# Attention turns its probabilities at another distance and in another order, and norms and the first up projection are interleaved by chunk

## The reference

```python
# first model, one layer (the context is updated in layer 0 only)
u  = modulate(rms_norm(h, g_norm1), mod[0], mod[1]);  uc = the same of the context
ya = diff_attention(...)                          # 4 heads of differences
yb = mla(...)                                     # 8 heads, latent: queries 64 + 32 rotary
yw = window_gqa(...)                              # 8 heads, window 128, with a sink
h  = h + mod[2] * merge_branches(u, (ya, yb, yw), ...)
u2 = modulate(rms_norm(h, g_norm2), mod[3], mod[4])
h  = h + mod[5] * conv_ffn(u2, w_up, conv_w, conv_b, w_down)

def mla_core(qn, qr, kn, kr, v):
    s = (q_nope . k_nope + q_rope . k_rope) * MLA_SCALE
    p = softmax(s);  return p @ v                 # 768 keys (512 + 256), context queries 256

def window_gqa(...):                              # blocks of 128 queries, keys: context + 3 blocks
    p = softmax_with_sink([s_context, s_band], sink);  return p @ v

def conv_ffn(t, w_up, conv_w, conv_b, w_down):
    a = dwconv(t @ w_up, conv_w, conv_b)          # w_up: 1024 x 5632
    gate, val = split(a);  return (silu(gate) * val) @ w_down

# second model, one layer
h = rmsnorm(x, attn_norm_w);  proj = h @ w_in
x = x + concat(ssd_mixer(...), short conv, nsa_mixer(...)) @ w_out    # 4 attention heads
h = rmsnorm(x, ffn_norm_w);   x = x + (silu(gate) * val) @ ffn_w_down
```

## Time and profile before

| | us |
|---|---|
| median of three runs | 4219.41 (4217.53 to 4221.92) |
| the profiled execution | 4218.24 |
| its span | 4216.5 |
| PE busy | 3872.1 (92% of the span) |
| DVE busy | 2300.0 (55%) |
| ACT busy | 1602.4 (38%) |
| POOL busy | 310.6 (7%) |

### The profile page before, as it was taken

One profiled execution on the slowest core, in us unless ns is written; L12 is line 12 of the kernel. 1 busy time (PEld: TensorE's weight loads), 2 busy tenths in 40 slices (PEclk: granted clock), 3 DMA queues, 4 the chain that ended last, 5 costly groups with the idle time before them and its releaser, 6 DMA issues. The chain is left out here.

```text
span 4216.5 us, 54188 instructions
## 1 busy us (share of the span) xinstructions
PE 3872.1 (92%) x20018; PEld 3044.8 (72%) x20018; DVE 2300.0 (55%) x3968; ACT 1602.4 (38%) x2718; POOL 310.6 (7%) x278
## 2 busy tenths in 40 slices
PE   4988979998999888999899899979899998989998
PEld 3875557776888787865678688856578886657886
DVE  6355567854553474364633556255657625565752
ACT  2245561112442353254632344243444424344431
POOL 0000001111000000100000100104010010400001
PEclk8999999999999999999999999989899999979999
DMA  5200005551223343200022233222023322202332
GB/s 175 61 28 19 1 22 172 193 191 56 95 95 105 99 160 114 77 28 19 1 90 85 78 97 95 99 67 83 13 80 98 97 94 83 80 16 87 98 99 81
DMA packets 86729, 350.83 MB, mean 83 GB/s; under 512 B 9520, under 2 KB 9648, under 8 KB 85680
## 3 DMA queue, kind: packets, MB, share of 16 engines
q1 hardware_dynamic: 72752, 298.53, 22.2%
q0 software_dynamic: 13824, 50.34, 3.6%
HBM read 346.73 MB, written 2.10 MB: 83 GB/s over the span
## 5 line engine op out<-in xcount | busy, mean ns | idle before, releaser
L498 DVE TENSOR_TENSOR split_low<-weight_ring,split_high 128x1024 fp32r<-128x1024 f32 (+2 forms) x460 | 623.0, 1355 | 677.6 <-ACT split_high L490 667.2
L490 ACT ACTIVATE split_high<-weight_ring 128x1024 fp32r<-128x1024 f32 (+2 forms) x474 | 535.0, 1130 | 918.1 <-PE banks L1460 468.8
L1632 PE MATMUL banks<-normed_high,split_high 128*128 128x512 f32 (+1 forms) x1760 | 653.8, 371 | 55.8 <-DVE normed_low L437 36.0
L1632 PE MATMUL banks<-normed_low,split_high 128*128 128x512 f32 (+1 forms) x1760 | 651.3, 370 | 0.0
L1632 PE MATMUL banks<-normed_high,split_low 128*128 128x512 f32 (+1 forms) x1760 | 650.6, 370 | 0.0
L1632 PEld LDWEIGHTS banks<-normed_high,split_high 128*128 128x128 f32 x1760 | 334.4, 190 | 117.5 <-issue 61.7
L1632 PEld LDWEIGHTS banks<-normed_low,split_high 128*128 128x128 f32 x1760 | 334.7, 190 | 55.8
L1632 PEld LDWEIGHTS banks<-normed_high,split_low 128*128 128x128 f32 x1760 | 334.6, 190 | 55.4
L1460 PE MATMUL banks<-hidden_high,split_high 128*128 128x512 f32 (+1 forms) x880 | 325.1, 369 | 8.8 <-DVE split_low L498 8.8
L1460 PE MATMUL banks<-hidden_low,split_high 128*128 128x512 f32 (+1 forms) x880 | 324.5, 369 | 0.0
L1460 PE MATMUL banks<-hidden_high,split_low 128*128 128x512 f32 (+1 forms) x880 | 324.3, 369 | 0.0
(11 more groups left out here) (327 smaller groups left out, 7228.7 us busy)
## 6 DMA issues: line engine op xcount, KB each, us to landing
weight_ring<-in_up SPq DMA_DIRECT2D x220, 512.0 KB, 3.6
weight_ring<-in_down SPq DMA_DIRECT2D x80, 704.0 KB, 4.0
modulation_ring<-in_ada POOLq DMA_DIRECT2D x80, 512.0 KB, 4.7
weight_ring<-in_merge SPq DMA_DIRECT2D x48, 768.0 KB, 4.4
weight_ring<-in_inputs SPq DMA_DIRECT2D x36, 512.0 KB, 3.5
weight_ring<-in_out SPq DMA_DIRECT2D x32, 512.0 KB, 3.6
latents<-in_ada POOLq DMA_DIRECT2D x16, 512.0 KB, 4.7
weight_ring<-in_xbc SPq DMA_DIRECT2D x16, 512.0 KB, 3.6
```

The lines of the kernel that those rows point to most:

```text
L490: act.activation(k.splits[0][:, (n0 + panel) % RING, 0:width], k.slot(n0 + panel)[:, 0:width], ACT.Copy).then_inc(k.high_ready.sem, 1)
L498: dve.tensor_tensor(k.splits[1][:, s, 0:width], k.ring[:, s, 0:width], k.splits[0][:, s, 0:width].bitcast(F32), ALU.subtract).then_inc(k.l ...
L1632: last = pe.matmul(sums(r, half), w, x, start=(c + j == 0), stop=(c == KT - 1 and j == 2))
```

## The change

Three parts.

1. In `norm`, DVE makes the low part of chunk i - 1 right after scaling chunk i (scaled 0, scaled 1, low 0, scaled 2, low 1, ..., scaled 7, low 6, low 7). This holds wherever a norm splits, in both models.
2. `attention` has a new argument. With `one_behind`, given to the latent attention alone, PE turns step t - 1 after the scores of step t, DVE normalises step t - 1 ahead of the maxima of step t, and ACT runs copy(t-1, 0), exponential(t, 0), exponential(t, 1), copy(t-1, 1). Without it the distance stays two, and ACT runs copy(t-2, 0), exponential(t, 0), copy(t-2, 1), exponential(t, 1). The difference attention has one copy per step and stays as it was.
3. `ffn_up` in the first model opens with a tile whose first four chunks go through both panels in turn, then chunks 4 to 7 of the first panel, then of the second. Tiles 0 and 1 are written out ahead of the loop, which runs 10 times for the rest. In the second model tiles 0 and 1 are written out too, in the order as before.

```diff
--- before.py
+++ after.py
@@ -414,6 +414,17 @@
         @block.vector
         def _(dve):
+            def low_part(q):
+                dst = flat[q][2][1]
+                dve.wait_ge(*k.high_ready(ahead + q + 1))
+                high = split[0][q].bitcast(F32)
+                if shifted:
+                    rest = dve.scalar_tensor_tensor(split[1][q], dst, flat[q][2][3](ranges_of[0][0][2]), high,
+                                                    ALU.add, ALU.subtract)
+                else:
+                    rest = dve.tensor_tensor(split[1][q], dst, high, ALU.subtract)
+                rest.then_inc(tile_ready.sem, 1)
+
...
-                for src, dst, gain, _ in group:
+                for i, (src, dst, gain, _) in enumerate(group):
                     for a, b, which in ranges_of[g]:
                         dve.scalar_tensor_tensor(dst[:, a:b], src[:, a:b], gain(which), k.probs[:, 3, a:b],
                                                  ALU.mult, ALU.mult).then_inc(k.scaled_ready.sem, 1)
-            for q, (_, _, (_, dst, _, _)) in enumerate(flat if split else ()):
...
+                    if split and i:
+                        low_part(tiles_before[g] + i - 1)
+            if split:
+                low_part(len(flat) - 1)
@@ -973,7 +978,7 @@
            constants_loaded=16)
-def attention(k, steps, turned, spare, scratch=None):
+def attention(k, steps, turned, spare, scratch=None, one_behind=False):
     nc = k.nc
@@ -982,6 +987,7 @@
     per = 1 if combined else 2
     slots = len(turned)
     groups = [sum(step["last"] for step in steps[:t]) for t in range(U)]
+    behind = 1 if one_behind else 2
@@ -1044,15 +1050,15 @@
-            for t in range(U + 3):
+            for t in range(U + behind + 1):
                 if t < U:
                     score(t)
-                if 2 <= t < U + 2:
-                    turn(t - 2, 0)
-                if t >= 3:
-                    weigh(t - 3)
-                if 2 <= t < U + 2 and per == 2:
-                    turn(t - 2, 1)
+                if behind <= t < U + behind:
+                    turn(t - behind, 0)
+                if t > behind:
+                    weigh(t - behind - 1)
+                if behind <= t < U + behind and per == 2:
+                    turn(t - behind, 1)
         @block.vector
         def _(dve):
@@ -1109,15 +1115,21 @@
-            for t in range(U + 3):
+            def normalise_both(t):
+                if 0 <= t < U:
+                    normalise(t, 0)
+                    normalise(t, 1)
+
+            for t in range(U + behind + 1):
+                if behind == 1:
+                    normalise_both(t - 1)
                 if t < U:
                     maximum(t, 0)
                     maximum(t, 1)
-                if 1 <= t <= U:
-                    normalise(t - 1, 0)
-                    normalise(t - 1, 1)
-                if t >= 3:
-                    store(t - 3)
+                if behind == 2:
+                    normalise_both(t - 1)
+                if t > behind:
+                    store(t - behind - 1)
@@ -1146,14 +1158,17 @@
-            for t in range(U + 2):
-                if t >= 2:
-                    copy(t - 2, 0)
+            for t in range(U + behind):
+                if t >= behind:
+                    copy(t - behind, 0)
                 if t < U:
                     exponential(t, 0)
+                    if behind == 1:
+                        exponential(t, 1)
+                if t >= behind and per == 2:
+                    copy(t - behind, 1)
+                if t < U and behind == 2:
                     exponential(t, 1)
-                if t >= 2 and per == 2:
-                    copy(t - 2, 1)
                 if scratch is not None and t >= 4:
                     square(t - 4)
             for t in range(U - 2, U) if scratch is not None else ():
@@ -1611,27 +1626,53 @@
     @block.tensor
     def _(pe):
-        with pe.Fori(0, FF_TILES // 2) as i:
-            for r in range(2):
+        def chunk(r, half, c):
+            for j, (w, x) in enumerate(triple(split_parts(k, n0, half, c * P), (highs[:, c, :], lows[:, c, :]))):
+                last = pe.matmul(sums(r, half), w, x, start=(c + j == 0), stop=(c == KT - 1 and j == 2))
+            return last
+
+        def sums_free(i, r):
+            if late is None:
+                pe.wait_ge(*k.taps_added(i * 8 + 4 * (r - 1)))
+            else:
+                pe.wait_ge(*k.scaled_ready(i * 4 + 2 * (r - 1)))
+            if late is not None and r == 1:
+                pe.wait_ge(*k.deviation_ready(0))
+
+        def opening_tile():
+            sums_free(0, 0)
+            for c in range(KT // 2):
+                pe.wait_ge(*k.normed_ready(c + 1 - KT))
                 for half in range(2):
-                    pe.wait_ge(*k.low_ready(i * 4 + (2 * r + half + 1)))
...
+                    if c == 0:
+                        pe.wait_ge(*k.low_ready(half + 1))
+                    chunk(0, half, c)
+            for half in range(2):
+                for c in range(KT // 2, KT):
+                    if half == 0:
+                        pe.wait_ge(*k.normed_ready(c + 1 - KT))
+                    last = chunk(0, half, c)
+                last.then_inc(k.product_ready.sem, 1)
+
+        def tile(i, r):
+            for half in range(2):
+                pe.wait_ge(*k.low_ready(i * 4 + (2 * r + half + 1)))
+                if half == 0:
+                    sums_free(i, r)
+                for c in range(KT):
+                    if r + half == 0:
+                        pe.wait_ge(*k.normed_ready(c + 1 - KT))
+                    last = chunk(r % 2, half, c)
+                last.then_inc(k.product_ready.sem, 1)
+
+        if late is None:
+            opening_tile()
+        else:
+            tile(0, 0)
+        tile(0, 1)
+        with pe.Fori(0, FF_TILES // 2 - 1) as i:
+            tile(i, 2)
+            tile(i, 3)
@@ -1844,7 +1885,7 @@
-    attention(k, steps, turned, [latents[:, 0, :], latents[:, 1, :]])
+    attention(k, steps, turned, [latents[:, 0, :], latents[:, 1, :]], one_behind=True)
```

More of the change, by code:

```diff
@@ L431, in _ @@
                                                  ALU.mult, ALU.mult).then_inc(k.scaled_ready.sem, 1)
-            for q, (_, _, (_, dst, _, _)) in enumerate(flat if split else ()):
-                dve.wait_ge(*k.high_ready(ahead + q + 1))
-                high = split[0][q].bitcast(F32)
-                if shifted:
-                    rest = dve.scalar_tensor_tensor(split[1][q], dst, flat[q][2][3](ranges_of[0][0][2]), high,
-                                                    ALU.add, ALU.subtract)
-                else:
-                    rest = dve.tensor_tensor(split[1][q], dst, high, ALU.subtract)
-                rest.then_inc(tile_ready.sem, 1)
+                    if split and i:
+                        low_part(tiles_before[g] + i - 1)
+            if split:
+                low_part(len(flat) - 1)
     squares = 0 if summed else len(flat)
```

14 lines of the change are left out of this document (removed).

## The result

The changed kernel takes 4173.64 us (median of four runs, 4172.29 to 4178.12) against 4218.66 us before in the same comparison: a ratio of 0.9889, interval 0.9877 to 0.9900. That is 45 us less.

What follows compares the result with a forecast made beforehand. TensorE (PE), busy 92% of the span, was taken as the bound, so only its waits pay. -10.6 - 4.0 - 8.8 - 9.1 + 4.0 = -28.5 us gave 4190.5 us; own range 4184 to 4196, 8 in 10 for 4179 to 4205.

Steps and rivals of the forecast that it cites:

- Window attention: Window attention, both layers: second copy ahead of the second exponential removes PE's waits; 10.6 us gained, between 7 and 13.
- Second model's attention: Second model's attention: the copy's new place saves 2.0 of 5.4 us per layer, 4.0 in all, bounds 0 and 7.
- a rival for the clock: Second model's attention: climb to the higher clock some 5 us later per layer, norm openings denser; -20, 4199 us, chance 0.09.
- Latent attention: Latent attention: distance one shortens fill and drain and keeps the clock up; 8.8 us gained, between 1.5 and 10.
- rival d: Latent attention: chain longer than a step's 6.05 us, so all 40 steps pay; +18, 4237 us, chance 0.03.
- the 1.6 us that I had for the clock: Latent attention's fill, per layer: without the second gap the clock stays up, saving an estimated 1.6 us.
- Openings: First model's feed-forward openings and the context's: earlier low parts start PE sooner; 9.1 us gained, between 6 and 11.
- the pairing is what makes this pay: First model's feed-forward opening: one panel at a time would starve PE, two panels paired would not; gain 3.8 us per layer.
- Second model's norms: Second model's norms: interleaving gains nothing and a clock fall costs 2 us per layer; +4 in all, between 0 and +5.
- job 2 would start when it did: Second model, after the first job: the next panel's split lands at about 2790.7, when the first job used to end.
- the fall of the clock in that gap: Second model's first job: a gap of 2 us lowers the clock, ten matmuls or so at double length, +2 us per layer.
- the 7 us of its upper bound: Second model's attention: most that the copy's new place was taken to gain there, 7 us in all.

Runs made afterwards that it cites:

- e10: Kernel before plus one extra 128-column matmul ahead of each turn in the second model's attention; 4212.15 us against 4221.45.
- e9: Changed kernel with distance two in the latent attention, keeping ACT's new order of the copies there; 4185.18 us, ratio 0.9907.
- e7: Changed kernel, but the first model's first feed-forward tile takes one panel after the other, without pairing; 4181.40 us.
- e11: Changed kernel plus one extra 128-column matmul ahead of each turn in the second model's attention; 4176.94 us, ratio 0.9898.
- e3: Changed kernel with the attention function of the kernel before, leaving only the norms by chunk and the opening tile; 4211.96 us, ratio 0.9975.
- e4: Changed kernel, but in the second model's attention only the iteration scoring step 2 has the new copy order, all later ones the old; 4193.60 us.
- e5: Changed kernel, but in the second model's attention the iteration scoring step 2 keeps the old copy order; 4173.69 us.

## Why the prediction was wrong, point by point

- **Window attention**: -9.7 us measured, -10.6 forecast. The anatomy of the earlier trace rows was read rightly. (Three stretches at 2.0 make 6.0, not the 5.8 of the sum.) In layer 1 the waits for the copy shrank by 3.5 us (6.0 to 2.5), less than the 4.8 I took, and the lower clock stood 5.8 us longer than before.
- **Second model's attention**: the step that failed. I priced a wait by its own length ("I take 2.0 of 5.4 per layer") and said of the lower clock only that PE "seldom waits" there, as if it were given. The waits did shrink by about 2 us per layer, but with them the clock's time at the lower level went from 49 to 30 and 26 us, which took another 6.6 and 7.7 us of PE's busy time. The lower clock was a result of the very waits, as e10 shows. So the term that I had at nothing was the clock's part of the gain: 14.3 us over both layers, beside the 3.6 us by which PE's idle time fell, near the 4.0 I had taken for it. I even had a rival for the clock, and gave it the wrong sign: that the climb would come later. (Its sum doesn't come out either: 28.5 less 5 less 1 is 22.5, not 20.)
- **Latent attention**: -8.2 against -8.8. Both ends and the hidden chain (rival d) came out as reckoned. That the clock stays up with the second gap gone is true in thirteen of eighteen fills, and was not in the very profile of layer 0. There the 1.6 us that I had for the clock didn't come, and the rest was 3.4 us where I had 2.6; that the total is near the forecast is in part luck. Read as a price, distance one also guards against falls such as those for which e9's slowest execution paid 5 and 6 us.
- **Openings**: -8.1 against -9.1; waits 3.8, 2.4 and 3.8 us shorter, as worked out, less 0.5 us each in the up projection, which the sum didn't have (0.4 us more lies in the matmuls ahead of the waits, by the cut of the stages). That "the pairing is what makes this pay" was too strong: e7 keeps two thirds without it.
- **Second model's norms**: +1.2 against +4.0. That job 2 would start when it did was right (the wait of 2.11 us); the fall of the clock in that gap, for which I had +2 per layer, didn't come in this profile. Elsewhere it did: in e11, e3 and e4 (layer 1) and in e7 (both layers) the clock fell for 3.4 us behind the same gap of 2.1 us, five of sixteen cases with this order, and the jobs up to the next gap took 1.6 us more. So the mechanism exists and was nearly the size I had given it, but it doesn't come each time.
- **Rivals and range**: no rival let the second model's attention gain more than the 7 us of its upper bound, so the range's lower end of 4179 was 5 us too high. Those bounds, 0 and 7 us, were taken from the waits alone.

## What to carry to other kernels

Where a stage runs at a mean clock well under one and PE has many short waits in it, don't price a wait by its length: count the time at the lower clock as well, and take half of it, the lower level being half of the higher, as the upper bound of what denser work can give back (here 18.8 and 23.2 us less at the lower clock, so 9.4 and 11.6 at most, and 6.6 and 7.7 measured). Read the clock's falls together with the waits, and part cause from company by adding work to PE, not only by taking waits away. Distance one paid where a step is longer than the chain behind its scores (6.05 against 4.8 us); whether it costs where the step is shorter stays open. And when a switch carries two choices with it, as the distance here carries the copy's place, compare with the kernel that shares the other one.

## What the runs showed of the hardware

More work made a stage shorter: 48 extra matmuls of 128 columns gave 5.4 and 4.9 us back. And the same instructions don't always meet the same clock. The latent attention with distance one, the same code in nine kernels, took 126.3 us in layer 0 where the clock never fell (five profiles) and 131.9 where it fell for 13.7 us. In the six kernels with the new order in the second model's attention (e5 counted, with its one iteration of the old order) that stage lay between 69.9 and 71.5 us in ten of twelve cases, and at 74.4 and 74.9 us in two. A difference of this size in one stage of two single profiles is no result.
